# Second iteration of each FFN: the product of plain blocks moved to third place, mixed blocks X7 and X4 made apart

## What is computed

```
def rmsnorm(x, g):
    xf = x.astype(jnp.float32)
    xf = xf * lax.rsqrt(jnp.mean(xf * xf, axis=-1, keepdims=True) + EPS)
    return xf.astype(x.dtype) * g

def swiglu(h, w_gate, w_up, w_down):
    return (jax.nn.silu(h @ w_gate) * (h @ w_up)) @ w_down

    h = h + 0.5 * swiglu(rmsnorm(h, ffn1_norm[l]), ffn1_w_gate[l], ffn1_w_up[l], ffn1_w_down[l])
```

## Time and profile before

| | us |
|---|---|
| median of 3 runs | 2546.14 (2545.93 to 2546.39) |
| the profiled execution | 2554.2 |
| its span, first to last instruction | 2552.1 |
| TensorE matmul busy | 2461.2 (96%) |
| VectorE busy | 1513.9 (59%) |
| ScalarE busy | 1474.5 (58%) |
| mean granted TensorE clock | 0.987 of full |

### The profile page before, as it was taken

One profiled execution on the slowest core, in us unless ns is written; L12 is line 12 of the kernel. 1 busy time (PEld: TensorE's weight loads), 2 busy tenths in 40 slices (PEclk: granted clock), 3 DMA queues, 4 the chain that ended last, 5 costly groups with the idle time before them and its releaser, 6 DMA issues. The chain is left out here.

```text
span 2552.1 us, 40112 instructions
## 1 busy us (share of the span) xinstructions
PE 2461.2 (96%) x16270; PEld 2236.6 (88%) x16270; DVE 1513.9 (59%) x2060; ACT 1474.5 (58%) x1911; POOL 418.0 (16%) x437
## 2 busy tenths in 40 slices
PE   6999999899999999999898999999989999999999
PEld 6999999899999899998678998877767888899998
DVE  6656656656566667565565565542996323665664
ACT  6456466464467565577555654754665645555644
POOL 0111110110111110111001111110764111011111
PEclk9999999899999999999999999999999999999999
DMA  6677693586687686888126867985435888578776
GB/s 179 168 192 170 177 228 80 147 206 160 172 204 187 153 201 164 191 211 208 29 61 165 224 154 183 229 184 117 116 91 127 184 193 193 120 178 202 179 184 158
DMA packets 250791, 425.35 MB, mean 167 GB/s; under 512 B 13024, under 2 KB 171360, under 8 KB 250608
## 3 DMA queue, kind: packets, MB, share of 16 engines
q0 software_dynamic: 53568, 195.06, 41.0%
q1 hardware_dynamic: 197040, 227.72, 27.8%
HBM read 225.60 MB, written 2.10 MB: 89 GB/s over the span
## 5 line engine op out<-in xcount | busy, mean ns | idle before, releaser
L783 PE MATMUL ps<-xbH,wH 128*128 128x256 f32 (+1 forms) x2800 | 796.0, 284 | 39.8 <-DVE xbL L1724 32.2
L783 PE MATMUL ps<-xbL,wH 128*128 128x256 f32 (+1 forms) x2800 | 794.1, 284 | 0.0
L783 PE MATMUL ps<-xbH,wL 128*128 128x256 f32 (+1 forms) x2800 | 793.3, 283 | 0.0
L595 POOL DMA_DIRECT2D wL<-raw x372 | 320.6, 862 | 2099.0 <-ACT wL L1180 2078.4
L1180 ACT ACTIVATE wL<-raw 128x1024 fp32r<-128x1024 f32 x372 | 392.8, 1056 | 308.0 <-PE ps L659 207.1
L783 PEld LDWEIGHTS ps<-xbH,wH 128*128 128x128 f32 x2800 | 532.8, 190 | 43.0 <-DVE xbL L1724 33.1
L783 PEld LDWEIGHTS ps<-xbL,wH 128*128 128x128 f32 x2800 | 531.7, 190 | 0.4
L783 PEld LDWEIGHTS ps<-xbH,wL 128*128 128x128 f32 x2800 | 532.0, 190 | 0.0
L1176 ACT ACTIVATE wH<-wS 128x1024 fp32r<-128x1024 f32 x200 | 212.2, 1062 | 509.9 <-DVE wS L1646 500.3
L1181 ACT ACTIVATE wH<-raw 128x1024 fp32r<-128x1024 f32 x375 | 392.5, 1047 | 2.2 <-DMA raw<-in_ffn_w_gate 2.0
L659 PE MATMUL ps<-aH,wH 128*128 128x264 f32 (+1 forms) x1232 | 352.5, 333 | 10.9 <-DVE m L1948 8.3
(11 more groups left out here) (293 smaller groups left out, 3261.1 us busy)
## 6 DMA issues: line engine op xcount, KB each, us to landing
wL<-raw POOLq DMA_DIRECT2D x372, 512.0 KB, 5.9
raw<-in_ffn_w_gate SPq DMA_DIRECT2D x88, 512.0 KB, 6.0
raw<-in_ffn_w_up SPq DMA_DIRECT2D x88, 512.0 KB, 6.7
raw<-in_ffn_w_down SPq DMA_DIRECT2D x88, 512.0 KB, 5.5
raw<-in_w_in SPq DMA_DIRECT2D x56, 512.0 KB, 4.0
raw<-in_w_ffn_in SPq DMA_DIRECT2D x44, 512.0 KB, 5.5
raw<-in_w_ffn_out SPq DMA_DIRECT2D x22, 512.0 KB, 5.3
raw<-in_w_o SPq DMA_DIRECT2D x12, 512.0 KB, 5.0
```

The source lines that it names most:

```text
L595: nc.gpsimd.dma_start(wL[:, u % RING, :], raw[:, UNITS[u].raw % RAW, :], accum_op=ALU.add).then_inc(lo_in[u % RING], 16)
L783: ins = nc.tensor.matmul(ps[:, 2 * s + j, 0:TH], lhs, rhs, start=p in (1, 5, 2) and k == q == 0, stop=p in (2, 3, 4) and k == KP - 1 and q ...
```

## The change

The second iteration of part 0 takes the products in the order `SECOND`. X7 and X4 get four short passes each instead of four double passes together. The ScalarE passes of X4 (and in f0 and f1 also those of X7) move from `first_gating` into `gating`, behind c5 or c6. Block 6 is made ahead of the statistics in f0 and f1. In `gating` VectorE's low parts, `hidden_low` of the first iteration and, in f2, the scales of the latent vectors change places in part 0.

```
+SECOND = (1, 5, 2, 6, 3, 7, 4)
 def turns(part, it):
-    return PLAIN if part == it == 0 else STEADY
+    if part == 0 and it < 2:
+        return (PLAIN, SECOND)[it]
+    return STEADY
...
-            mixes[f] = [place(f"mix{f}{i}", [P, 2, T // 2], F32, a_at + (FMAX + 4 + i) * T * 4) for i in range(2)]
+            mixes[f] = place(f"mix{f}", [P, KP, T // 2], F32, a_at + (FMAX + 4) * T * 4)
...
@@ ScalarE @@
+            def block47(f, n):
+                for k in range(KP):
+                    on_dve(f"t{n}:f{f}:{k}")
+                    fn(nc.scalar.activation(blocks[f][0][:, XI[n], k, :], mixes[f][:, k, :], ACT.Copy,
+                                            scale=-1.0), f"x{n}h:f{f}:{k}")
...
@@ ScalarE, first_gating @@
+                for k in range(KP):
+                    block6(f, k)
                 if f < 2:
+                    high(u + RING, f"{st}:0:g1.1")
+                    high(u + 1 + RING, f"{st}:0:g2.1")
                     root(f"f{f}", T)
+                    silu()
                     on_pe(f"{st}:0:u1.1")
                     for k in range(KP):
                         block5(f, k, gain)
                     high(u + 2 + RING, f"{st}:0:u1.1")
                     high(u + 3 + RING, f"{st}:0:u2.1")
                 else:
                     if f > 2:
                         root(f"f{f}", T)
+                    high(u + RING, f"{st}:0:g1.1")
                     high(u + 1 + RING, f"{st}:0:g2.1")
                     silu()
                     high(u + 2 + RING, f"{st}:0:u1.1")
                     for k in range(KP):
                         block5(f, k, gain)
+                    block47(f, 7)
                     high(u + 3 + RING, f"{st}:0:u2.1")
...
@@ ScalarE, gating @@
+                    if part == 0 and p == 5:
+                        block47(f, 7 if f < 2 else 4)
+                    if part == 0 and p == 6 and f < 2:
+                        block47(f, 4)
...
@@ VectorE @@
+            def sum4(f, k, gain):
+                on_act(f"x7h:f{f}:{k}")
+                do(V.scalar_tensor_tensor(mixes[f][:, k, :], rows(f, KP + k)[:, 0, :], gcol(*gain, KP + k),
+                                          sixes[f][:, k, :], ALU.mult, ALU.subtract), f"t4:f{f}:{k}")
+            def mix47(f, n, gain):
+                bH, bL = (t[:, XI[n], :, :] for t in blocks[f])
                 own()
+                for k in range(KP):
+                    (sum7 if n == 7 else sum4)(f, k, gain)
+                for k in range(KP):
+                    on_act(f"x{n}h:f{f}:{k}")
+                    do(V.scalar_tensor_tensor(bL[:, k, :], mixes[f][:, k, :], -1.0, f32(bH[:, k, :]),
+                                              ALU.mult, ALU.subtract), f"x{n}:f{f}:{k}")
...
@@ VectorE, first_gating, f < 2 @@
                     sums(u + RING, f"{name}:g1.1")
+                    scales(f"f{f}", T)
                     gates()
+                    sums(u + 2 + RING, f"{name}:u1.1")
                     low(u + RING)
                     for k in range(KP):
                         block5(f, k, gain)
                     ups()
                     sums(u + 3 + RING, f"{name}:u2.1")
                     low(u + 2 + RING)
...
@@ VectorE, gating @@
                     sums(u + i + RING, done)
+                    if part == 0 and p == 1:
+                        lows(u + i + RING)
+                    if part == 0 and p == 5:
+                        lows(u + i + RING)
+                        if f < 2:
+                            mix47(f, 7, gain)
+                        mix47(f, 4, gain)
                     if p == 3:
...
+                        if part == 0:
+                            hidden_low(f, before)
...
-                        if f == 2 and part == 0 and it == 1:
-                            latent_scales("kv", RKV, T1)
+                    if f == 2 and (part, it, p) == (0, 1, 4):
+                        latent_scales("kv", RKV, T1)
```

More of the change, by code:

```diff
@@ L1262, in silu @@
                         fn(nc.scalar.activation(t2[:, j, 0:T], t1[:, j, 0:T], ACT.Silu), f"{st}:0:silu{j}")
+                for k in range(KP):
+                    block6(f, k)
                 if f < 2:
+                    high(u + RING, f"{st}:0:g1.1")
+                    high(u + 1 + RING, f"{st}:0:g2.1")
                     root(f"f{f}", T)
-                    high(u + RING, f"{st}:0:g1.1")
+                    silu()
                     on_pe(f"{st}:0:u1.1")
@@ L1269, in first_gating @@
                         block5(f, k, gain)
[L1270 to L1273, removed]
                     high(u + 2 + RING, f"{st}:0:u1.1")
-                    block47(f, 0)
-                    block47(f, 1)
                     high(u + 3 + RING, f"{st}:0:u2.1")
-                    block47(f, 2)
-                    block47(f, 3)
-                else:
-                    for k in range(KP):
-                        block6(f, k)
-                    high(u + RING, f"{st}:0:g1.1")
+                else:
                     if f > 2:
                         root(f"f{f}", T)
+                    high(u + RING, f"{st}:0:g1.1")
                     high(u + 1 + RING, f"{st}:0:g2.1")
                     silu()
-                    block47(f, 0)
-                    block47(f, 1)
                     high(u + 2 + RING, f"{st}:0:u1.1")
@@ L1701, in sum6, with sum7 @@
                                           ALU.mult, ALU.add), f"t6:f{f}:{k}")
[L1703 to L1710, removed]
+            def sum7(f, k, gain):
+                do(V.scalar_tensor_tensor(mixes[f][:, k, :], rows(f, k)[:, 1, :], gcol(*gain, k), u12s[f][:, k, :],
                                           ALU.mult, ALU.subtract), f"t7:f{f}:{k}")
+            def sum4(f, k, gain):
+                on_act(f"x7h:f{f}:{k}")
+                do(V.scalar_tensor_tensor(mixes[f][:, k, :], rows(f, KP + k)[:, 0, :], gcol(*gain, KP + k),
+                                          sixes[f][:, k, :], ALU.mult, ALU.subtract), f"t4:f{f}:{k}")
             def block6(f, k):
@@ L1718, in block6 @@
                                           f32(bH[:, XI[6], k, :]), ALU.mult, ALU.subtract), f"x6:f{f}:{k}")
[L1720 to L1728, removed]
-                own()
[L1731 to L1734, removed]
+            def mix47(f, n, gain):
+                bH, bL = (t[:, XI[n], :, :] for t in blocks[f])
+                own()
+                for k in range(KP):
[4 more added lines that the diff above has]
+                                              ALU.mult, ALU.subtract), f"x{n}:f{f}:{k}")
             def prep_blocks(k):
@@ L1820, in first_gating @@
                     sum6(f, k, gain)
+                for k in range(KP):
+                    block6(f, k)
                 if f < 2:
-                    variance(f"f{f}", T, D)
                     sums(u + RING, f"{name}:g1.1")
-                    rsqrt(rs[:, 0:T], var[:, 0:T], sd[:, 0:T], f"sd:f{f}")
+                    scales(f"f{f}", T)
                     own()
                     gates()
-                    sums(u + 1 + RING, f"{name}:g2.1")
+                    sums(u + 2 + RING, f"{name}:u1.1")
                     low(u + RING)
[L1829 to L1851, removed]
                     for k in range(KP):
@@ L1856, in first_gating, with gating @@
                     low(u + 2 + RING)
-                    mix47(f, (2, 3), gain)
+                else:
+                    if f > 2:
+                        variance(f"f{f}", T, D)
+                    sums(u + RING, f"{name}:g1.1")
+                    if f > 2:
+                        rsqrt(rs[:, 0:T], var[:, 0:T], sd[:, 0:T], f"sd:f{f}")
+                        own()
+                    gates()
+                    sums(u + 2 + RING, f"{name}:u1.1")
+                    low(u + RING)
+                    for k in range(KP):
+                        block5(f, k, gain)
+                    mix47(f, 7, gain)
+                    ups()
+                    sums(u + 3 + RING, f"{name}:u2.1")
+                    low(u + 2 + RING)
                 return name
-            def gating(f, part, it, before):
+            def gating(f, part, it, before, gain):
                 st = f"gu{f}{part}"
@@ L1879, in gating @@
                         up_first(f, before)
-                    elif p == 5 and before:
+                    elif p == 5 and before and part:
                         hidden_low(f, before)
@@ L1884, in gating @@
                             on_act(before + ":ah")
+                            own(before + ":lo")
                         for j in range(2):
@@ L1910, in gating @@
                         do(V.tensor_tensor(m[:, :, TH:T], m[:, :, TH:T], t2[:, :, TH:T], ALU.mult), f"up:{name}")
-                    lows(u + i + RING)
+                    if part or p not in (1, 5):
+                        lows(u + i + RING)
+                    if f == 2 and (part, it, p) == (0, 1, 4):
+                        latent_scales("kv", RKV, T1)
```

(2 more changed lines are left out.)

2 lines of the change are left out of this document (removed).

## The result

The changed kernel took 2533.91 us (median of 8 runs, 2530.55 to 2538.34), the kernel before 2547.44 beside it (8 runs, 2542.57 to 2556.22): ratio 0.9948, 95% interval 0.9932 to 0.9965, some 13 us faster. The forecast was 26.2. Run again later, it gave 0.9937 (0.9915 to 0.9958), 16 us. The two profiled executions lie 19.4 us apart (2554.2 and 2534.8). Executions of one kernel differ by up to 18 us, so stages are read from these two traces and sums from the ratios.

A forecast was written before the change was run, and what follows sets the result against it. Prediction: PE's idle time bounds the kernel, product 6 waiting for c1, queued on ACT behind X4 and X7. Gains 7.9 + 7.0 + 3.1 + 4.5 + 3.7 = 26.2 from 2546.1 give 2519.9 us; range 2509 to 2538.

The forecast's parts named there:

- The waits around the products: Part 0, f0 and f1: the 9.96 us before product 6 goes; 1.8 for c6, 5.0 for `u22` come; gain 3.3 each.
- the short waits: Products in f2 to f4: waits of 1.1 us instead of 3.4 to 4.5, too short for a slow stretch.
- f1 as f0 over again: FFN f1 was given f0's wait of 10.0 us before product 6 and the same gain of 3.3 us.
- The down projection's wait: Down projection of part 0: gone in f0 and f1, some 5 us in f3, 1 to 3 in f2 and f4.
- the landing in f2: `w_up` load in f2: lands between 7.5 and 16.6 us after issue, 14 taken; new wait 1.9, gain 3.1.
- the landing in f4: `w_up` load in f4: was just in time, comes 3.7 us earlier while PE comes 5.8 earlier; gain 3.7.
- the clock: PE at about half clock after waits: 1.9 us in f0 and f1, 2.6 in f2 to f4, 1.7 for down waits.
- A: Rival on loads: every `w_up` load takes 7.5 to 12 us; 35 us gained, 2511; chance 0.17.
- B: Rival on PE's clock: a slow stretch follows each new wait, 16.7 us given back, gain 9.5, 2537; chance 0.20.
- C: Rival, no effect: X4's path holds product 4 in f0, f1; loads take all of f2 to f4; within 5 us; 0.09.
- D: Rival on the load queue: the load falls behind a further add, landing from 21 us on; 26 slower, 2572; chance 0.09.

The follow-up runs named there:

- c1 first: Kernel before, with ScalarE's last two double passes of the mixed blocks moved behind the copy c1, nothing else: 2554.3 us, 1.0010.
- drains first: Changed kernel, with the weight sum of part 1 moved behind the first four drains of the down projection in part 0: 2512.89 us, 0.9852.
- order only: Kernel before, with the second iteration's new product order and the sums and low parts it needs moved, mixed blocks as before: 2554.75 us, 1.0019.
- c1 first with drains: Kernel before, with the last two mixed-block passes behind c1 and the four drains ahead of the weight sum: 2532.07 us, 0.9920.
- all three: Changed kernel, with the edits of drains first, add held and X4 sooner together: 2506.4 us, 0.9828.
- add held: Changed kernel, GpSimd issuing the burst's fourth add only once the second `w_up` tile has landed, which holds back three adds: 2514.67 us, 0.9856.
- X4 sooner: Changed kernel, in f0 and f1 X4's ScalarE passes moved ahead of unit 12 and `hidden_low` ahead of the mixed blocks: 2527.25 us, 0.9907.
- order with drains: Kernel before, with the new product order, its two weight sums moved, and the four drains ahead of the weight sum: 2523.89 us, 0.9889.
- drains alone in the kernel before: Kernel before, with only the weight sum for the next part's product 5 moved behind the first four drains in part 0: 0.9950.

## Why the prediction was half right

**The waits around the products: right in the mechanism.** c1 behind X4 and X7 was the true bound (c1 first), product 2 in between covers it, and the new waits stand where the working put them: `u22` 5.0 forecast, 5.12 and 5.14 measured; c6 1.8 forecast, 1.96 in f0, but 0.27 in f1 and 0.45 in f0 when it was run again. In f2 to f4 the short waits add up to 0.3, 1.1 and 1.7 (1.1 forecast for each), and f2's down projection came 4.9 us earlier (5.0 forecast). f0 and f1 together gave 15.0 us against 14.9, but that is luck: f0 gave 1.4 less and f1 1.5 more than forecast. I took f1 as f0 over again, with two units and the table load ahead of the root, and f1's root waits for neither; in f0 product 4 started at 63.37 instead of 62.2, and its slow stretch cost 2.4 instead of 1.9.

**The down projection's wait: the step that failed.** The mechanism was forecast (earlier products meet a load that comes no earlier), its size was not. Forecast were waits of 1.9 in f2, some 5 in f3 and 5.8 - 3.7 = 2.1 in f4, 9.0 together, with no slow clock behind them. Measured: 5.16, 4.55 and 4.51, 14.2, and 7.05 of slow clock. That is 12.3 more. By FFN, in us gained:

| | f0 | f1 | f2 | f3 | f4 | sum |
|---|---|---|---|---|---|---|
| forecast | 7.9 | 7.0 | 3.1 | 4.5 | 3.7 | 26.2 |
| the two traces | 6.5 | 8.5 | -2.7 | 4.9 | -0.35 | 16.9 |

All of the shortfall of 9.3 is in f2 and f4. In f3 the slow clock of 1.7 was made good by a term that I didn't have, also found in f4: the wait for c6 early in part 1 fell from 1.61 to 0.32 in f3 and from 1.42 to 0.26 in f4. So 26.2 - 12.3 = 13.9 comes close to the medians' 13.5 in part by chance. Three terms were mis-sized:
- the landing in f2, 14 taken, 16.4 measured, and the issue 0.9 later than worked out. I had both ends (7.5 and 16.6) and the closer adds as a reason for the upper one, and still took less;
- the landing in f4, moved along with the 12.4 us that it took before, measured 15.6;
- the clock. I charged a slow stretch to the down waits that vanished (1.7 each) and none to those that stayed or came, because f3's 3.48 had none. One stretch without is no rule: the price of a wait must be the same on both sides of the sum.

**The rivals.** A (loads land early) fell: 15.3 to 16.4 in f2 to f4. It is what holding the adds makes true, 7.4, 8.1 and 7.6, and the time follows. B (slow clock behind each new wait) was half true: in the changed kernel not behind the c6 wait, but behind `u22` and all three down waits; 2537 was nearer than my forecast. Behind the c6 wait it differs from run to run: 1.00 again with the adds held, 0.57 with the drains first. C fell in the products and nearly holds by its second half, the loads and the slow clock leaving 1.9 us of gain in f2 to f4. D (the load delayed by a further add's worth, 21 us or more) is in none of the stretches read; the longest landing of a `w_up` load there is 17.7.

With the fourth add and the two behind it held back, the load lands in half the time; what is under way beside it in the other queue decides. The Trainium skill ("DMA: Bandwidth & Descriptors", Queues, rings and completion order), which has each DMA engine take turns between its queues packet by packet, agrees, and its reading for this change, every load near 16.6, came true within 1.3 us. I gave it 1.2 us in f2 and left f4 out. Both were too little: by my own sum (850.5 + 16.6 + 2.2 = 869.3 against 869.8) a landing of 16.6 leaves 0.5 us of gain in f2, 2.6 less than the 3.1, and in f4 it takes 4.2 more.

**Still open.** At 1135.57 PE waits 2.46 us, since ACT waited 9.38 for the load of `w_dq`, not so in the kernel before. It was there again when the kernel was run again (2.28), in the order only (2.19), c1 first with drains (2.27) and all three (2.21), with 1.20 in drains first and 1.06 in add held. It is not in X4 sooner, c1 first or the order with drains, and hardly with the drains alone in the kernel before (0.27), so it follows none of the edits plainly. Over this stretch (1062 to 1275) the changed kernel loses 2.3 us; that was in no term, and what sets it is open.

## What to carry to other kernels

When a stage is made to start earlier, follow the next wait for a transfer through to its end in every repetition of the stage, and give each the landing time of the most crowded row, not the one it happened to have. An in-order engine that does work for later ahead of a drain turns a late prefetch into a stall: put the drain first. Here that cost some 2.6 us of later waits in the changed kernel, and in the kernel before it was worth about as much (13 us) as the change alone (13 to 16). Charge a wait its slow clock when it comes as when it goes. And where a stage is repeated, look in each repetition for what is not the same, here a table load that only f0 has.

## What the runs showed of the hardware

The granted clock behind a wait does not follow from the wait's length alone. In the kernel before it was 1.00 behind the 3.48 us of f3:

```profile
1373.50:1379.50 6.00, 5.95 (x24) 4.39 (x25) 5.59 (x8) 0.26 (x1) 0.00 (x0) 1.00 0.05 14
```

and 0.66 behind f0's 2.86; after the change it stayed 1.00 behind 1.96 us at 55, while with X4 sooner it fell to 0.57 behind 1.89 us at 60:

```profile
60.00:64.00 4.00, 3.66 (x17) 3.69 (x18) 1.13 (x3) 3.21 (x5) 1.32 (x2) 0.57 1.11 293
```

With the drains first, whose program is the same up to there, the same wait at 55 was 1.94 us long, and the clock behind it was 0.57 instead of 1.00. The 24 matmuls of product 7, done in 3.16 us above, are then not done in 4:

```profile
55.00:59.00 4.00, 4.00 (x20) 4.00 (x21) 1.86 (x5) 4.00 (x8) 0.86 (x1) 0.57 0.98 157
```

And with X4 sooner it was 1.00 behind 2.01 us in f1, where it was 0.57 behind 1.89 in f0. So for waits of some 2 to 3.5 us one trace does not tell whether a slow stretch follows:

```profile
450.50:454.50 4.00, 3.97 (x32) 4.00 (x33) 1.42 (x2) 2.75 (x5) 0.86 (x1) 1.00 1.08 274
```

Behind the waits of over 4 us the stretches read were between 0.50 and 0.72. A 512 KB load took 7.4 us with one adding DMA of the same size beside it for most of that time, and 16.4 with two or three beside it for most of the time: a factor of 2.2.
